# Hybrid layer, output stage: one clearing block less, W_out slots 6 and 7 split by ScalarE and VectorE, order of the first two tiles' projections

## The chip, the cores and the metric

The kernel runs on one core of a Trainium2 chip. The metric is device time in microseconds (us), the median of several runs. A core has five engines with a queue each: TensorE (PE; its weight loads are shown as PEld), VectorE (DVE), ScalarE (ACT), GpSimd (POOL) and SyncE (SP), which here only issues DMAs. They run side by side and wait for one another through semaphores.

## What is computed

One decoder layer on x of 2048 tokens by 1024, in float32:

```python
u  = rmsnorm(x, pre_mix_gain)
p  = u @ w_in                                   # rg_x, rg_gate, q, k, v, o, i, f
y_rg = rmsnorm(rg_lru(conv4(rg_x)) * gelu(rg_gate), rg_out_gain)
y_ml = rmsnorm(sigmoid(o) * mlstm(silu(conv4(q)), silu(conv4(k)), v, i, f), ml_out_gain)
h = x + rmsnorm(concat(y_rg, y_ml) @ w_out, post_mix_gain)
v = rmsnorm(h, pre_mlp_gain)
out = h + rmsnorm(relu(v @ w_up) ** 2 @ w_down, post_mlp_gain)
```

The change touches only the way from y = concat(y_rg, y_ml) to h and v, and what lies between the stages.

## The kernel before

**Stages.** Three parts follow one another: build_prepare (norm, transposes), build_mixers (projection and both mixers, which write y to HBM as a high and a low part) and build_output. Each opens a block of its own with a program for each engine, and a block ends with a barrier of all engines. Behind each of the first two stands clear_semaphores (L1666), a block in which each engine clears a fifth of the semaphores, again with a barrier at its end; then the semaphores are handed out anew.

**Products.** Every product is made of three matmuls: high by high, high by low, low by high (L1350 to L1352, one call each). A float32 weight tile in w_raw is split for it: w_hi is the rounded copy (L1319 on GpSimd, L1520 on ScalarE), w_lo = w_raw - w_hi (L1321). A weight lies in 8 slots of 128 x 1024; slot i uses w_raw[i % 2], so slot i + 2 is loaded (L1297, by GpSimd's queue) when slot i is split.

**Output stage.** It goes twice over 8 token tiles of 128 (B = 0: tiles 0 to 7, B = 1: tiles 8 to 15). Each pass has a projection phase with W_out, then 8 rounds of the MLP (chunk), of which each needs 8 new slots. split_round (L1299) is GpSimd's program for one such set of slots. For B = 0, slots 0 to 5 of W_out were split during the mixers and only 6 and 7 are left to it. For B = 1, slots 4 to 7 are still in use by the last MLP round, so GpSimd does 0 to 3 early; after that round ScalarE makes w_hi of 4 to 7 (L1520), and GpSimd w_lo.

**One tile's projection.** project(B, i, b, part) (L1355) is 24 matmuls: part 0 uses slots 0 to 3 and writes the bank rg_ps, part 1 slots 4 to 7 and ml_ps. It waits for the tile's y (y_in, loaded by SP, L1219), for the slots (w_split) and, last, until its bank has been emptied of the tile before. There is one bank pair for each part. ScalarE empties rg_ps with scale_rg (L1468), which writes h1_t; VectorE empties ml_ps with the sum L1586 (signal "mix"). scale_rg of tile 0 of a pass stands ahead of tile_steps (L1522 in ScalarE's program, behind the high parts of slots 4 to 7 and final_square when B = 1); for each later tile it stands in the middle of the tile before's steps.

**A tile's steps.** VectorE and ScalarE by turns: sum L1586, square sum L1451, root L1456, scale L1593, residual L1599, square sum and root again, v_t (L1607). TensorE transposes v_t (L1374) after the tile after next's part 0, ScalarE copies the high part (L1494), VectorE makes the low part (L1619). In the second pass VectorE and ScalarE also finish the first pass's tiles in between (L1451 on acc, L1564, L1570), SP stores them (L1228) and loads what is needed of the next (L1238), in one queue with the loads of y for the tile after next.

**TensorE's order.** Tiles 0 and 1 of a pass: part 0 and part 1 of tile 0, then of tile 1. Then a loop: part 0 of tile T + 2, transposes of tile T, part 1 of tile T + 2. Then the last transposes and the MLP rounds. GpSimd begins to split the first MLP round's slots when part 0 of the pass's last tile is done.

Of the kernel before, what the change touches and what calls it, by code (L numbers as in the profile page):

```python
# [23 lines left out]
F32 = mybir.dt.float32  # L24
F32R = mybir.dt.float32r
ALU = mybir.AluOpType
ACT = mybir.ActivationFunctionType
# [1116 lines left out]
def build_output(nc, a, k, out):  # L1144
# [4 lines left out]
    NF = DFF // (FC * P)  # L1149
    HALVES = 2  # L1150
    SLOTS = 8
    with ExitStack() as ctx:
# [12 lines left out]
        w_hi = [t[:].rearrange("p k f -> p (k f)") for t in k["w_hi"]] + [sb(f"w_hi{i}", [P, D], F32R)[:] for i in (6, 7)]  # L1165
        w_lo = [t[:].rearrange("p k f -> p (k f)") for t in k["w_lo"]] + [sb(f"w_lo{i}", [P, D], F32R)[:] for i in (6, 7)]
        w_raw = [sb(f"w_raw{i}", [P, D]) for i in range(2)]
# [30 lines left out]
        w_split = [sem(f"w_split{i}") for i in range(SLOTS)]  # L1198
        raw_in = k["raw_in_o"]
# [9 lines left out]
        def raw_count(r, i):  # L1209

            return r * 64 + ((i // 2 + 1) * 16 - 48)
# [68 lines left out]
        @block.gpsimd  # L1280
        def _(pool):
            up = a["mlp_w_up"][0].rearrange("(k p) f -> p k f", p=P)
            down = a["mlp_w_down"][0]
            w_out = a["w_out"][0]

            def source(rnd, f, i):
                if rnd == "out":
                    return w_out[i * P:(i + 1) * P, :]
                if i < FC:
                    return up[:, :, ds(f * (FC * P) + i * P, P)]  # L1290
                return down[ds(f * (FC * P) + (i - FC) * P, P), :]

            def load_raw(rnd, f, i):
                dst = w_raw[i % 2][:]
                if rnd != "out" and i < FC:
                    dst = dst.rearrange("p (k f) -> p k f", k=KT)
                pool.dma_start(dst, source(rnd, f, i)).then_inc(raw_in[i % 2], 16)  # L1297

            def split_round(B, rnd, f):  # L1299
                r = f + (B * (NF + 1) + (rnd != "out"))  # L1300
                first = 6 if rnd == "out" and B == 0 else 0
                load_raw(rnd, f, first)
                load_raw(rnd, f, first + 1)
                for i in range(first, SLOTS):
                    pool.wait_ge(raw_in[i % 2], raw_count(r, i))
                    if rnd == "out":
                        if B and i < FC:
                            pool.wait_ge(s_slot[f"up_used{i}"], s_slot.ready(B * NF - 1))
                        elif B:
                            pool.wait_ge(s_dn["dn_mm"], s_dn.ready(B * NF * 2 * TB - 1))  # L1310
                    else:
                        if i < FC:
                            pool.wait_ge(s["mm_rg"], s.ready(B * TB + TB - 1))
                            pool.wait_ge(s_slot[f"up_used{i}"], f + (B * NF + 1))
                        else:
                            pool.wait_ge(s_y["mm_ml"], s_y.ready(B * TB + TB - 1))
                            pool.wait_ge(s_dn["dn_mm"], (f + B * NF) * (2 * TB) + s_dn.credit)
                    if not (rnd == "out" and B and i >= FC):
                        pool.tensor_tensor(w_hi[i], w_raw[i % 2][:], one_bc, ALU.mult).then_inc(w_split[i], 1)  # L1319
                    pool.wait_ge(w_split[i], r * 2 + 1)  # L1320
                    pool.tensor_tensor(w_lo[i], w_raw[i % 2][:], w_hi[i].bitcast(F32), ALU.subtract  # L1321
                                       ).then_inc(w_split[i], 1)
                    if i + 2 < SLOTS:
                        pool.wait_ge(w_split[i], r * 2 + 2)
                        load_raw(rnd, f, i + 2)
                for i in (SLOTS - 2, SLOTS - 1):
                    pool.wait_ge(w_split[i], r * 2 + 2)

            one_bc = k["one"][:].broadcast_to([P, D])
            for i in range(6):  # L1330
                pool.sem_inc(w_split[i], 2)
            for B in range(NB):
                split_round(B, "out", 0)
                with pool.Fori(0, NF) as f:
                    split_round(B, "mlp", f)

        @block.tensor
        def _(pe):
# [16 lines left out]
            def project(B, i, b, part):  # L1355
                T = i + B * TB
                r = B * (NF + 1)
                bank, evac, done = ((rg_ps, "mix_rg", s["mm_rg"]), (ml_ps, "mix", s_y["mm_ml"]))[part]
                ks = range(part * 4, part * 4 + 4)
                pe.wait_ge(y_in[b], (T // 2 + 1) * 32)  # L1360
                for c in ks:
                    pe.wait_ge(w_split[c], r * 2 + 2)
                pe.wait_ge(s[evac], s.freed(T))
                for h in range(HALVES):
                    cols = slice(h * 512, (h + 1) * 512)
                    last = product(bank[:, h, :], [(y_hi[b][:, c, :], y_lo[b][:, c, :], w_hi[c][:, cols],
                                                    w_lo[c][:, cols]) for c in ks])
                last.then_inc(done, 1)
# [45 lines left out]

            for B in range(NB):
                T0 = B * TB
                for i in range(2):
                    project(B, i, i, 0)
                    project(B, i, i, 1)
                if B:  # L1420
                    pe.wait_ge(s_dn["add"], s_dn.ready(B * NF * 16 - 1))
                with pe.Fori(0, TB // 2 - 1) as j:
                    for b in range(2):
                        i = j * 2 + (2 + b)
                        project(B, i, b, 0)
                        transposes(j * 2 + (T0 + b))
                        project(B, i, b, 1)
                transposes(T0 + TB - 2)

                def last_transposes():  # L1430
                    transposes(T0 + TB - 1)

                    pe.wait_ge(s["sq2"], s.ready(T0 + TB - 1))

                chunk(B, 0, last_transposes)
                with pe.Fori(1, NF) as f:
                    chunk(B, f)

        @block.scalar
        def _(act):  # L1440
# [70 lines left out]
            act.wait_ge(rg_scale, 1)  # L1511
            nc.scalar.activation(stat["s_rg"][:], stat["t_rg"][:], ACT.Sqrt).then_inc(rg_scale, 1)
            act.wait_ge(rg_scale, 3)
            for B in range(NB):
                if B:
                    act.wait_ge(s_dn["add"], s_dn.ready(B * NF * 16 - 1))

                    for i in range(FC, SLOTS):
                        act.wait_ge(raw_in[i % 2], raw_count(B * (NF + 1), i))
                        nc.scalar.activation(w_hi[i], w_raw[i % 2][:], ACT.Copy).then_inc(w_split[i], 1)  # L1520
                    final_square(B - 1, 0)
                scale_rg(B, 0, 0)  # L1522
                tile_steps(B, 0, 0, before=False)
                with act.Fori(0, TB // 2 - 1) as j:
                    for b in (1, 0):
                        tile_steps(B, j * 2 + (1 if b else 2), b)
                tile_steps(B, TB - 1, 1, after=False)
                tile_evac(B, TB - 1)
                for b in range(2):
                    act.wait_ge(h1_out[b], (B + 1) * (TB // 2) * 16)  # L1530
                if B:
                    ready("fo", B * TB - 1)
                with act.Fori(0, NF) as f:
                    chunk(B, f)
# [8 lines left out]
        def _(dve):  # L1543
# [105 lines left out]
            dve.wait_ge(rg_scale, 2)  # L1649
            nc.vector.reciprocal(stat["s_rg"][:], stat["s_rg"][:]).then_inc(rg_scale, 1)  # L1650
            for B in range(NB):
                tile_steps(B, 0, 0, before=False)
                with dve.Fori(0, TB // 2 - 1) as j:
                    for b in (1, 0):
                        tile_steps(B, j * 2 + (1 if b else 2), b)
                tile_steps(B, TB - 1, 1)
                tile_evac(B, TB - 1)
                if B:
                    dve.wait_ge(fin_out, 16 * TB)
                chunk(B, 0, True)  # L1660
                with dve.Fori(1, NF if B < NB - 1 else NF - 1) as f:
                    chunk(B, f, False)
# [39 lines left out]
def hybrid_layer(nc, a, out):  # L1702
    with ExitStack() as ctx:
# [46 lines left out]
        with ExitStack() as sems:  # L1750
            k["sems"] = sems
            build_mixers(nc, a, k)
            clear_semaphores(nc, k)
        mixer_consts.close()
        with ExitStack() as sems:
            k["sems"] = sems
            build_output(nc, a, k, out)


# [17 lines left out]
```

## Time and profile before

| what | us |
|---|---|
| median of 3 runs (2466.47 to 2467.31) | 2466.69 |
| the profiled execution | 2467.44 |
| its span | 2465.6 |
| TensorE busy | 2335.1 (95%) |
| VectorE busy | 1278.3 (52%) |
| GpSimd busy | 834.4 (34%) |
| ScalarE busy | 642.5 (26%) |

The mixers end at 822.8 us of the span, the first pass's projections run from 835.1 to about 957, its MLP rounds to 1634; the second pass's projections from 1634 (with a gap) to about 1777, its MLP rounds to 2456. Times in the rows are in us from the span's start. In rows of the timeline the second column is the duration, and the square brackets at the end tell how long the engine was idle before, and what ended that. Matmuls are pipelined, so their durations overlap.

### The profile page before, as it was taken

How to read it: one execution, taken by the hardware profiler on the slowest of the kernel's cores; microseconds unless marked ns; L12 is line 12 of the kernel's file. 1: busy time of each engine (PE TensorE's matmuls, PEld its weight loads, DVE VectorE, ACT ScalarE, POOL GpSimd, SP SyncE). 2: the span in 40 equal slices, each digit the busy share in tenths (PEclk: the TensorE clock that was granted, in tenths of full speed). 3: DMA queues.
4: the chain of work that ended last, by engine and by line, in shares of the span. 5: the costliest groups of instructions: out<-in, count | busy, mean ns of one | idle time of the engine just before them, and what ended most of it. 6: DMA issues, size and time to landing. Idle time of an engine off the chain costs nothing.

```text
span 2465.6 us, 29981 instructions
## 1 busy us (share of the span) xinstructions
PE 2335.1 (95%) x10696; PEld 1943.9 (79%) x10696; DVE 1278.3 (52%) x1584; ACT 642.5 (26%) x1159; POOL 834.4 (34%) x486
## 2 busy tenths in 40 slices
PE   5779999999999599999999999979899999999998
PEld 5758888888887487888888888868688888888886
DVE  5345665656656256445435444517755434534535
ACT  3315554545545232001101101114201101100112
POOL 8400000000000108536435534610746534633630
PEclk9689999999999799999999999989899999999999
DMA  4634453635542552112111101327412111101203
GB/s 171 245 119 153 149 190 121 218 122 174 165 165 71 170 163 94 43 52 68 34 43 60 51 34 51 102 98 244 144 51 69 43 42 51 60 27 50 68 17 145
DMA packets 125177, 254.85 MB, mean 103 GB/s; under 512 B 8105, under 2 KB 43137, under 8 KB 125121
## 3 DMA queue, kind: packets, MB, share of 16 engines
q1 hardware_dynamic: 97008, 157.37, 19.0%
q0 software_dynamic: 24320, 88.35, 11.4%
q10 hardware_dynamic: 3792, 8.47, 0.9%
q8 instruction: 24, 0.39, 0.1%
q14 instruction: 33, 0.26, 0.0%
HBM read 201.67 MB, written 50.40 MB: 102 GB/s over the span
## 4 chain that ended last, share of the span: by engine, by line
PE 60%; DVE 3%; issue 1%; ACT 1%; DMA 1%; POOL 0%; ACTq 0%; DVEq 0%; SPq 0%; PEldq 0%; POOLq 0%
PE o_ps L1350 20%; PE o_ps L1352 20%; PE o_ps L1351 20%; DVE o_relu L1626 1%; DVE o_ff_lo L1630 1%; ACT o_ps L1451 1%; PE o_ps L1374 0%; DMA o_v_lo<-ylo_d 0%; DVE o_acc L1570 0%; DVE o_v_lo L1619 0%; DMA o_w_raw<-in_w_out 0%; DVE o_h_t L1586 0%; ACT o_ff_hi L1508 0%; DVE o_h_t L1599 0%; DVE o_v_t L1607 0%
## 5 line engine op out<-in xcount | busy, mean ns | idle before, releaser
L1319 POOL TENSOR_TENSOR w_hi<-o_w_raw,one 128x1024 fp32r<-128x1024 f32 x100 | 191.7, 1917 | 685.2 <-PE o_ps L1352 594.7
L1350 PE MATMUL o_ps<-o_v_hi,w_hi 128*128 128x512 f32 x1024 | 400.1, 391 | 4.8 <-DVE o_v_lo L1619 4.8
L1351 PE MATMUL o_ps<-o_v_lo,w_hi 128*128 128x512 f32 x1024 | 399.6, 390 | 0.0
L1352 PE MATMUL o_ps<-o_v_hi,w_lo 128*128 128x512 f32 x1024 | 399.6, 390 | 0.0
L1640 DVE TENSOR_TENSOR o_acc<-o_ps,o_acc 128x512 f32<-128x512 f32 x224 | 154.2, 690 | 377.5 <-PE o_ps L1352 377.2
L658 PE MATMUL m_unit_ps<-u_hi,w_hi 128*128 128x512 f32 x768 | 309.4, 403 | 6.3 <-issue 6.3
L1626 DVE TENSOR_TENSOR o_relu<-o_relu 128x512 f32<-128x512 f32 x128 | 218.8, 1710 | 182.7 <-ACT o_relu L1505 181.7
L1505 ACT ACTIVATE o_relu<-o_ps 128x512 f32<-128x512 f32 x128 | 76.5, 597 | 874.9 <-PE o_ps L1352 843.3
L658 PE MATMUL m_unit_ps<-u_hi,w_lo 128*128 128x512 f32 x768 | 301.5, 393 | 0.0
L658 PE MATMUL m_unit_ps<-u_lo,w_hi 128*128 128x512 f32 x768 | 299.9, 390 | 0.0
L1630 DVE TENSOR_TENSOR o_ff_lo<-o_relu,o_ff_hi 128x512 fp32r<-128x512 f32 x128 | 243.1, 1899 | 90.8 <-ACT o_ff_hi L1508 90.8
L1321 POOL TENSOR_TENSOR w_lo<-o_w_raw,w_hi 128x1024 fp32r<-128x1024 f32 x102 | 274.1, 2688 | 47.2 <-ACT w_hi L1520 39.4
L1350 PEld LDWEIGHTS o_ps<-o_v_hi,w_hi 128*128 128x128 f32 x1024 | 193.1, 189 | 45.4 <-issue 5.3
L1352 PEld LDWEIGHTS o_ps<-o_v_hi,w_lo 128*128 128x128 f32 x1024 | 193.0, 188 | 40.2
L1351 PEld LDWEIGHTS o_ps<-o_v_lo,w_hi 128*128 128x128 f32 x1024 | 193.0, 189 | 40.1
L1350 PE MATMUL o_ps<-w_hi,o_ff_hi 128*128 128x512 f32 x512 | 199.3, 389 | 1.4 <-DVE o_acc L1637 1.4
L1352 PE MATMUL o_ps<-w_hi,o_ff_lo 128*128 128x512 f32 x512 | 199.2, 389 | 0.0
L1350 PE MATMUL o_ps<-o_w_hi,o_ff_hi 128*128 128x512 f32 x512 | 199.2, 389 | 0.0
L1352 PE MATMUL o_ps<-o_w_hi,o_ff_lo 128*128 128x512 f32 x512 | 199.2, 389 | 0.0
L1351 PE MATMUL o_ps<-o_w_lo,o_ff_hi 128*128 128x512 f32 x512 | 199.2, 389 | 0.0
L1351 PE MATMUL o_ps<-w_lo,o_ff_hi 128*128 128x512 f32 x512 | 199.2, 389 | 0.0
L615 POOL DMA_DIRECT2D w_raw<-in_w_in x18 | 15.9, 885 | 482.6 <-DVE w_lo L1075 462.4
(255 smaller groups left out, 3639.5 us busy)
## 6 DMA issues: line engine op xcount, KB each, us to landing
o_w_raw<-in_mlp_w_up POOLq DMA_DIRECT2D x64, 512.0 KB, 4.7
o_w_raw<-in_mlp_w_down POOLq DMA_DIRECT2D x64, 512.0 KB, 3.6
u_hi<-uhi_d SPq DMA_DIRECT2D x14, 2048.0 KB, 10.6
u_lo<-ulo_d SPq DMA_DIRECT2D x14, 2048.0 KB, 15.0
w_raw<-in_w_in POOLq DMA_DIRECT2D x24, 512.0 KB, 4.8
p_xu<-in_x SPq DMA_DIRECT2D x16, 512.0 KB, 7.9
uhi_d<-u_hi SPq DMA_DIRECT2D x4, 2048.0 KB, 7.5
ulo_d<-u_lo SPq DMA_DIRECT2D x4, 2048.0 KB, 13.1
```

What stands on the lines that cost most here:

```text
L615: pool.dma_start(w_raw[c % 3][:], w_view[:, :, ds(g * P + W_COL[UNITS[c]], P)]).then_inc(raw_in[c % 3], 16)
L658: last = nc.tensor.matmul(unit_bank[u][:], w[u][:, c, :], x[:, b, c, :], start=(c == 0 and z == 0), stop=(c == KT - 1 and z == 2))
L1319: pool.tensor_tensor(w_hi[i], w_raw[i % 2][:], one_bc, ALU.mult).then_inc(w_split[i], 1)
L1321: pool.tensor_tensor(w_lo[i], w_raw[i % 2][:], w_hi[i].bitcast(F32), ALU.subtract).then_inc(w_split[i], 1)
L1350: nc.tensor.matmul(dst, sh, mh, start=(i == 0), stop=False)
L1351: nc.tensor.matmul(dst, sh, ml, start=False, stop=False)
L1352: last = nc.tensor.matmul(dst, sl, mh, start=False, stop=(i == n - 1))
L1451: nc.scalar.activation(junk, src, ACT.Square, accum_out=stat["ss" + n][:, ds(T, 1)]).then_inc(s["sq" + n], 1)
L1505: nc.scalar.activation(relu[n % 2][:], ps[:, n % 4, :], ACT.Relu).then_inc(s_up["relu"], 1)
L1626: nc.vector.tensor_tensor(relu[n % 2][:], relu[n % 2][:], relu[n % 2][:], ALU.mult).then_inc(s_ff["ffsq"], 1)
L1630: nc.vector.tensor_tensor(ff_lo[:, i, cols], relu[n % 2][:], ff_hi[:, i, cols].bitcast(F32), ALU.subtract).then_inc(s_ff["fflo"], 1)
L1640: nc.vector.tensor_tensor(dst, ps[:, 4 + n % 4, :], dst, ALU.add).then_inc(s_dn["add"], 1)
```

## The change

Three things are changed. The clearing block behind the mixers is gone: the output stage takes new semaphores beside those of the mixers. In both rounds of W_out GpSimd leaves slots 6 and 7 alone (it still loads them and waits until they are split); ScalarE makes the high part (new for B = 0, as before for B = 1) and VectorE the low part, ahead of its first tile. And TensorE projects part 0 of tiles 0 and 1 of a pass, then part 1 of both.

```diff
--- before.py
+++ after.py
@@ -1302,6 +1302,9 @@
                 load_raw(rnd, f, first)
                 load_raw(rnd, f, first + 1)
                 for i in range(first, SLOTS):
+                    if rnd == "out" and i >= SLOTS - 2:
+                        pool.wait_ge(w_split[i], r * 2 + 2)
+                        continue
                     pool.wait_ge(raw_in[i % 2], raw_count(r, i))
                     if rnd == "out":
                         if B and i < FC:
@@ -1414,9 +1417,9 @@
 
             for B in range(NB):
                 T0 = B * TB
-                for i in range(2):
-                    project(B, i, i, 0)
-                    project(B, i, i, 1)
+                for part in range(2):
+                    for i in range(2):
+                        project(B, i, i, part)
                 if B:
                     pe.wait_ge(s_dn["add"], s_dn.ready(B * NF * 16 - 1))
                 with pe.Fori(0, TB // 2 - 1) as j:
@@ -1511,6 +1514,9 @@
             act.wait_ge(rg_scale, 1)
             nc.scalar.activation(stat["s_rg"][:], stat["t_rg"][:], ACT.Sqrt).then_inc(rg_scale, 1)
             act.wait_ge(rg_scale, 3)
+            for i in (SLOTS - 2, SLOTS - 1):
+                act.wait_ge(raw_in[i % 2], raw_count(0, i))
+                nc.scalar.activation(w_hi[i], w_raw[i % 2][:], ACT.Copy).then_inc(w_split[i], 1)
             for B in range(NB):
                 if B:
                     act.wait_ge(s_dn["add"], s_dn.ready(B * NF * 16 - 1))
@@ -1649,6 +1655,10 @@
             dve.wait_ge(rg_scale, 2)
             nc.vector.reciprocal(stat["s_rg"][:], stat["s_rg"][:]).then_inc(rg_scale, 1)
             for B in range(NB):
+                for i in (SLOTS - 2, SLOTS - 1):
+                    dve.wait_ge(w_split[i], B * (NF + 1) * 2 + 1)
+                    nc.vector.tensor_tensor(w_lo[i], w_raw[i % 2][:], w_hi[i].bitcast(F32), ALU.subtract
+                                            ).then_inc(w_split[i], 1)
                 tile_steps(B, 0, 0, before=False)
                 with dve.Fori(0, TB // 2 - 1) as j:
                     for b in (1, 0):
@@ -1750,10 +1760,7 @@
         with ExitStack() as sems:
             k["sems"] = sems
             build_mixers(nc, a, k)
-            clear_semaphores(nc, k)
-        mixer_consts.close()
-        with ExitStack() as sems:
-            k["sems"] = sems
+            mixer_consts.close()
             build_output(nc, a, k, out)
```

## Rows read from the trace of the kernel before

**Rows 1.** The page, part 1: busy time of the engines.
```profile
PE 2335.1 (95%) x10696; PEld 1943.9 (79%) x10696; DVE 1278.3 (52%) x1584; ACT 642.5 (26%) x1159; POOL 834.4 (34%) x486
```

**Rows 2.** Table by stretches: length, busy time per engine, granted clock, DMA share, GB/s.
```profile
840.00:845.00 5.00, 5.00 (x22) 4.13 (x21) 0.00 (x0) 1.12 (x1) 2.58 (x3) 0.94 1.01 379
...
955.00:960.00 5.00, 2.58 (x13) 2.01 (x12) 3.01 (x2) 2.11 (x4) 4.25 (x4) 1.00 0.30 105
...
1646.00:1652.00 6.00, 0.00 (x0) 0.00 (x0) 0.00 (x0) 4.15 (x5) 4.51 (x2) 0.50 0.20 80
```

**Rows 3.** Lines of both barriers and TensorE's clears: count, ns min/median/max, starts.
```profile
L500 SPq EVENT_SEMAPHORE  x1: 17/17/17, 822.8 to 822.8; - x1
...
L1669 PEldq DRAIN  x2: 13/13/13, 139.0 to 825.1; - x2
L1669 SPq EVENT_SEMAPHORE  x2: 17/17/17, 139.2 to 825.3; - x2
...
L1688 PEldq EVENT_SEMAPHORE_RANGE_CLEAR  x25: 56/56/63, 138.2 to 825.0; - x25
```

**Rows 4.** Timeline, start of the output stage: start, duration, engine, line, operation.
```profile
825.86 0.58 SPq L1219 DMA_DIRECT2D o_v_hi<-yhi_d  x1
...
828.70 3.40 SPq L1219 DMA_DIRECT2D o_v_lo<-ylo_d  x1
...
835.09 0.79 PE L1350 MATMUL o_ps<-w_hi,o_v_hi 128*128 128x512 f32 x1 [16.89 <-DMA o_v_lo<-ylo_d]
...
838.38 2.36 POOL L1321 TENSOR_TENSOR o_w_lo<-o_w_raw,o_w_hi 128x1024 fp32r<-128x1024 f32 x1
```

**Rows 5.** Timeline, tiles 0 and 1 of the first pass.
```profile
843.51 1.12 ACT L1468 ACTIVATE o_h_t<-o_ps,o_s_rg 128x1024 f32<-128x1024 f32 x1 [15.80 <-PE o_ps L1352]
...
848.99 1.23 DVE L1586 TENSOR_TENSOR o_h_t<-o_ps,o_h_t 128x1024 f32<-128x1024 f32 x1 [20.99 <-PE o_ps L1352]
...
853.38 1.23 DVE L1599 TENSOR_TENSOR o_h_t<-o_h_t,o_xh 128x1024 f32<-128x1024 f32 x1
...
857.13 1.29 DVE L1607 SCALAR_TENSOR_TENSOR o_v_t<-o_h_t,o_rs,o_pre_mlp 128x1024 f32<-128x1024 f32 x1
859.76 1.23 DVE L1586 TENSOR_TENSOR o_h_t<-o_ps,o_h_t 128x1024 f32<-128x1024 f32 x1 [1.35 <-PE o_ps L1352]
```

**Rows 6.** Timeline between the passes: ScalarE, GpSimd, TensorE.
```profile
1648.53 1.06 ACT L1520 ACTIVATE o_w_hi<-o_w_raw 128x1024 fp32r<-128x1024 f32 x1 [1.21 <-DMA o_w_raw<-in_w_out]
...
1650.53 1.09 ACT L1468 ACTIVATE o_h_t<-o_ps,o_s_rg 128x1024 f32<-128x1024 f32 x1
...
1647.49 4.64 POOL L1321 TENSOR_TENSOR o_w_lo<-o_w_raw,o_w_hi 128x1024 fp32r<-128x1024 f32 x2 [4.84 <-ACT o_w_hi L1520]
...
1652.39 0.77 PE L1350 MATMUL o_ps<-w_hi,o_v_hi 128*128 128x512 f32 x1 [12.84 <-POOL o_w_lo L1321]
```

**Rows 7.** Timeline, tiles 8 and 9: VectorE's first sums, ScalarE's wait.
```profile
1660.12 1.23 DVE L1586 TENSOR_TENSOR o_h_t<-o_ps,o_h_t 128x1024 f32<-128x1024 f32 x1 [25.19 <-PE o_ps L1352]
...
1665.46 1.12 ACT L1468 ACTIVATE o_h_t<-o_ps,o_s_rg 128x1024 f32<-128x1024 f32 x1 [2.42 <-PE o_ps L1352]
...
1670.90 1.23 DVE L1586 TENSOR_TENSOR o_h_t<-o_ps,o_h_t 128x1024 f32<-128x1024 f32 x1 [0.21 <-PE o_ps L1352]
```

**Rows 8.** Timeline, end of the second pass's projections, all engines.
```profile
1723.41 0.82 SPq L1219 DMA_DIRECT2D o_v_lo<-ylo_d  x1
...
1730.00 0.49 PE L1350 MATMUL o_ps<-w_hi,o_v_hi 128*128 128x512 f32 x1 [0.21 <-DMA o_v_lo<-ylo_d]
...
1733.82 1.22 DVE L1586 TENSOR_TENSOR o_h_t<-o_ps,o_h_t 128x1024 f32<-128x1024 f32 x1
...
1735.97 1.89 POOL L1319 TENSOR_TENSOR w_hi<-o_w_raw,one 128x1024 fp32r<-128x1024 f32 x1 [81.22 <-PE o_ps L1352]
...
1739.14 3.14 DVE L1599 TENSOR_TENSOR o_h_t<-o_h_t,o_xh 128x1024 f32<-128x1024 f32 x1
...
1750.34 1.94 PE L1374 MATMUL o_ps<-ident,o_v_t 128*128 128x128 f32 x8 [8.24 <-DVE o_v_lo L1619]
```

## The prediction

> **Names.** A token tile is 128 tokens; tiles 0 to 7 are the first pass of the output stage (B = 0), tiles 8 to 15 the second (B = 1). The first half of a tile's projection is slots 0 to 3 of W_out into the rg bank, the second half slots 4 to 7 into the ml bank. 0.2% of 2466.7 us is 4.9 us, about what a measurement of this kernel can tell from no change.
>
> **What bounds the kernel now.** I read the page first: TensorE is busy 95% of the span [rows 1], so only a place where it waits, or a wait that the change adds, can move the time. Then the waits of PE and the table by stretches [rows 2], then the timeline around each place that the diff touches. Three places matter. (1) Between the mixers and the output stage TensorE is idle for 16.89 us, and its first matmul waits for the DMA of tile 0's low part, not for a weight slot [rows 4]. (2) Between the passes it is idle for 12.84 us, until GpSimd has split slot 7 [rows 6]. (3) After that the second pass is set by the chain of VectorE and ScalarE, one tile in (1733.82 - 1670.90) / 5 = 12.58 us [rows 7, 8], which ends in 8.24 us of idle TensorE ahead of tile 14's transposes [rows 8]. In the first pass VectorE waits for TensorE at each tile (1.35 us at tile 1) [rows 5], so there TensorE sets the pace. The MLP rounds are TensorE's, and nothing in them is touched.
>
> **Part 1, the clearing block.** SP leaves the mixers' barrier at 822.8 and the clearing block's at 825.3; TensorE is the late one, 25 clears of 56 ns each over both blocks and a drain at 825.1 [rows 3]. Nothing computes in that time and the loads of the output stage begin 0.5 us after it, at 825.86 [rows 4]. All DMA of the mixers has landed (the barrier follows the wait for it), so the loads find the same empty queues, only earlier. Price: -2.5 us. Bounds: 0, if what follows were held by something else, and -2.5.
>
> **Part 2, slots 6 and 7 in the first pass.** GpSimd ends its last split at 838.38 + 2.36 = 840.7 [rows 4]; the slots are first needed at the second half of tile 0, after 843.5 [rows 5]. The split by ScalarE (1.06 us for the high part of a slot [rows 6]) and VectorE (1.23 us for a sum of two 128x1024 tiles in SBUF [rows 5]) ends sooner, about 834, in both engines' idle time. Price: 0. GpSimd gets free earlier and loads the first two MLP tiles (1 MB) among SP's loads; tile 1's low part, asked for at 828.7, must now be there at about 842 instead of 849, with over 10 us in hand.
>
> **Part 3, the order of the halves in the first pass.** Each bank holds one tile. Before, TensorE left the rg bank, worked 5.5 us on the ml bank (843.51 to 848.99), and the rg bank had long been emptied when it came back. Now the first half of tile 1 comes right behind that of tile 0 and must wait until ScalarE has emptied the bank: 1.12 us [rows 5] and some 0.15 us for the two hand-overs = 1.3 us. In the same way the second half of tile 1 comes right behind that of tile 0 and waits for VectorE's sum: 1.23 us [rows 5] + 0.15 us = 1.4 us. These 2.7 us lie on TensorE, which sets the pace of this pass: +2.7 us. (The 0.15 us are an estimate, of which the lower bound is 0 and the upper the 0.26 us that TensorE took to start behind GpSimd's split, 1652.39 - (1647.49 + 4.64) [rows 6].) Tile 0's sum is now 5.5 + 2.7 us later against TensorE's start, so its chain to v_t, 848.99 to 858.42 [rows 5], ends at about 862.5; its transposes come at about 865.6, so this costs nothing, and VectorE's delay of 2 us at tile 1 melts by some 0.3 us a tile, since TensorE is the slower one. First pass together: -2.5 + 2.7 = +0.2 us.
>
> **Part 4, the second pass.** This is where I expect the loss. ScalarE's program is: high parts of slots 4 to 7, the square of the last accumulated tile, and only then the emptying of the rg bank, 1650.53 to 1651.62 [rows 6]. The first half of tile 8 was done at 1652.4 - 12.8 = 1639.6 [rows 6] and sits in that bank. So the first half of tile 9, now second in line, can't start before about 1651.7: it can't use the 12 idle us. And since it stands ahead of the second half of tile 8, whose slots are ready at 1650.9 (ScalarE ends slot 7's high part at 1649.59 [rows 6], VectorE needs 1.23 us instead of GpSimd's 2.35), it delays it. The gain of the faster split, 1652.1 - 1650.9 = 1.2 us, is not used either.
> Sum: the first project after the idle stretch runs partly at the lower clock and takes 1660.12 - 1652.39 = 7.7 us [rows 6, 7]; the next 5.5 us. Second half of tile 8 done: 1651.7 + 7.7 + 5.5 = 1664.9 instead of 1660.1, +4.8 us. VectorE's chain of tile 8, and with it the whole chain of this pass, begins 4.8 us later. Two things are taken back. VectorE's 0.21 us wait ahead of tile 9's sum goes [rows 7]; and ScalarE no longer sits 2.42 us in front of tile 9's bank [rows 7], since that half is finished early, which brings tile 8's second square some 0.3 us forward. +4.8 - 0.5 = +4.3 us. Bounds: +3.8 (the same chain with 1 us of slack found) and +4.8.
> The wait for tile 8's sum ahead of tile 9's second half (1.4 us) is hidden here, since the chain is the slower one. Does the +4.3 reach the end? TensorE has no lead in this pass that could grow: tile 15's first half waited 0.21 us for a load [rows 8] that SP issues behind the store of a final tile, so behind VectorE's chain. It moves by the same 4.3 us, and with it GpSimd's first MLP split, 1735.97, which follows that half. So VectorE's chain meets GpSimd in the same phase as before, tile 14's transposes come at 1750.34 + 4.3 (+0.2), and from there TensorE sets the pace to the end, as before.
>
> **Sum.** +0.2 + 4.3 = +4.5 us. The profiled execution has a span of 2465.6 and took 2467.4, 1.8 us around it; it is 0.75 us above the median of the runs. Span after: 2470.1, its time about 2472.0. On the median: 2466.7 + 4.5 = **2471.2 us**, +0.18%, just inside the bound of 4.9 us.
>
> **Where the port between VectorE and GpSimd comes in.** A VectorE sum with both inputs in SBUF, 1.23 us alone, took 3.14 us while GpSimd split a slot [rows 5, 8]. If the tile-15 half did not wait for its load, GpSimd would start 2 us earlier against VectorE's chain; stepping through the rows with whole instructions blocking one another, tile 14's v_t then ends anywhere from 2.1 to 4.8 us later than before, instead of 4.3. The Trainium skill, page "SBUF — State Buffer", section "Who interferes with whom", says that such a VectorE instruction and one of GpSimd that reads SBUF exclude each other for a whole instruction, and that issue order decides who waits; the 3.14 us agree.
>
> **Rivals.**
> (a) Slower by over 0.2%: the same mechanism, a little dearer. The first project of the output stage ran some 13 matmuls at the lower clock (835.09 to 840.4) [rows 4, 2], the one at 1652.39 only 9 or 10, at 0.20 us each. If tile 9's first half gets 13, +0.8 us; if the 0.5 us of slack do not come, +0.5 us. 2471.7 to 2472.5. It decides from 0.4 us on. For: the terms are only known to a few tenths, and all that remains open in part 4 is slack. Against: the first pass may in turn save 0.8 us. Chance 0.27.
> (b) The clearing block was cover for something, such as loads or instruction code, and the first matmul does not move: +7.0 us, 2473.7. For: TensorE's wait ends with a DMA. Against: that DMA is issued 0.5 us after the barrier. Chance 0.06.
> (c) The two stalls of 1.3 us in the first pass come just after the clock has risen, and it falls again: 24 matmuls of a half at 0.20 us more each, +4.8 us, 2476.0. Against: from 955 to 960 TensorE was idle 2.4 of 5 us and the granted clock stayed at 1.00 [rows 2]. Chance 0.05. The Trainium skill, page "TensorE: Matmul & The Clock Gate", section "A second HAM failure mode: psum-queue depth-cycling", tells of short idle times between groups of matmuls, from cycling through PSUM banks, between which the clock went up and down; the row of 955 to 960 does not agree, so the case keeps a small chance.
> (d) The port's phase is kinder, as above: +2.3 instead of +4.5, 2469.0. Needs the load of tile 15 to be early. Chance 0.12.
> (e) The change does what its order suggests: tile 9's first half runs in the idle stretch, and tile 8's second half starts at 1651.0 at the upper clock. Then -1.4 - 2.2 + 0.2 = -3.4 us, 2463.3. Against: the place of the bank's emptying in ScalarE's program. Chance 0.04; faster by over 0.2% needs still more, 0.04.
> Forecast 0.42.
>
> **How the numbers follow.** Within 0.2%: forecast, (d), (e) = 0.58. Slower: (a), (b), (c) = 0.38. Faster: 0.04. Range: from (d) with 0.4 us less to just past (b): 2468.6 to 2474.0. It leaves out (c), (e) and the faster case, 0.13, and strays.
>
> **What would show it.** First load of the output stage at 823.4. TensorE idle 1.3 us behind the first half of tile 0, for ScalarE's emptying, and 1.4 us behind its second half, for VectorE's sum. Between the passes TensorE idle about 12.2 us, ended by ScalarE's emptying of the rg bank, not by a split, and VectorE's first sum of the pass some 4.8 us later against the end of the first pass. Wrong, if tile 9's first half starts before 1651, if the wait at 1651.7 is ended by a weight slot, or if the gap ahead of tile 14's transposes takes up the loss.

## The result

| kernel | median us | runs | ratio of its runs to before | 95% interval |
|---|---|---|---|---|
| before | 2467.86 | 15 | | |
| changed | 2471.69 | 15 | 1.0017 | 1.0009 to 1.0025 |
| changed, measured again (e9) | 2471.88 | 11 | 1.0022 | 1.0013 to 1.0031 |

The change costs 3.8 us by the medians, 2.2 to 6.2 by the interval of the first comparison: slower beyond the noise, by about 0.2%; on which side of 0.2% it lies, neither interval tells. The prediction was +4.5 us.

The profiled execution of the changed kernel is one of the slowest: 2475.64 us, span 2473.9, which is 8.3 us above that of before. So the two traces are compared from two points that the change does not touch: R, the mixers' last root (L844, 815.89 before, 817.85 after), and E, VectorE's last accumulation of a pass's MLP rounds (1634.23 before, 1638.58 after).

**Where TensorE waits after.** The waits of TensorE in the changed kernel from 1600 on (engine, line, who it waited for: us in total, times, longest), then its waiting rows of the first pass in the timeline, with ScalarE's and VectorE's that end them:

```profile
PE o_ps L1353 <- ACT o_h_t L1471: 12.2, 1, 12.2
PE o_ps L1377 <- DVE o_v_lo L1625: 8.3, 1, 8.3
PE o_ps L1353 <- DVE o_v_lo L1625: 2.4, 1, 2.4
PE o_ps L1353 <- DMA o_v_lo<-ylo_d: 2.0, 4, 0.8
PE o_ps L1353 <- DVE o_h_t L1592: 1.5, 1, 1.5
```

```profile
825.35 0.59 SPq L1219 DMA_DIRECT2D o_v_hi<-yhi_d  x1
...
834.52 0.80 PE L1353 MATMUL o_ps<-w_hi,o_v_hi 128*128 128x512 f32 x1 [14.35 <-DMA o_v_lo<-ylo_d]
...
841.63 0.39 PE L1355 MATMUL o_ps<-w_hi,o_v_lo 128*128 128x512 f32 x1
843.31 0.47 PE L1353 MATMUL o_ps<-w_hi,o_v_hi 128*128 128x512 f32 x1 [1.30 <-ACT o_h_t L1471]
843.62 0.40 PE L1354 MATMUL o_ps<-w_lo,o_v_hi 128*128 128x512 f32 x1
...
855.96 0.47 PE L1353 MATMUL o_ps<-w_hi,o_v_hi 128*128 128x512 f32 x1 [1.51 <-DVE o_h_t L1592]
...
842.05 1.11 ACT L1471 ACTIVATE o_h_t<-o_ps,o_s_rg 128x1024 f32<-128x1024 f32 x1 [7.43 <-PE o_ps L1355]
...
854.59 1.23 DVE L1592 TENSOR_TENSOR o_h_t<-o_ps,o_h_t 128x1024 f32<-128x1024 f32 x1 [18.70 <-PE o_ps L1355]
```

The first load stands 7.5 us behind R (825.35 - 817.85) instead of 10.0, the first matmul 16.7 instead of 19.2 [rows 4]. Then come two waits that before did not have [rows 5]: 1.30 us until ScalarE has emptied the rg bank, 1.51 us until VectorE's sum has emptied the ml bank. TensorE loses more than these idle times, because matmuls in a row overlap: they start 0.23 us apart, across the first wait 843.31 - 841.63 = 1.68 us, and the next one comes 0.31 us later. That is 1.5 us for the first wait, and in the same way 1.8 us for the second (854.06 to 855.96 and 856.26): 3.3 us for the two.

**Between the passes and at the end of the second.** Timeline rows, as in [rows 6 to 8]:

```profile
1654.86 1.09 ACT L1471 ACTIVATE o_h_t<-o_ps,o_s_rg 128x1024 f32<-128x1024 f32 x1
...
1653.95 1.22 DVE L1660 TENSOR_TENSOR o_w_lo<-o_w_raw,o_w_hi 128x1024 fp32r<-128x1024 f32 x1 [0.91 <-ACT o_w_hi L1526]
...
1656.10 0.77 PE L1353 MATMUL o_ps<-w_hi,o_v_hi 128*128 128x512 f32 x1 [12.21 <-ACT o_h_t L1471]
...
1669.63 1.22 DVE L1592 TENSOR_TENSOR o_h_t<-o_ps,o_h_t 128x1024 f32<-128x1024 f32 x1 [14.46 <-PE o_ps L1355]
...
1679.81 1.22 DVE L1592 TENSOR_TENSOR o_h_t<-o_ps,o_h_t 128x1024 f32<-128x1024 f32 x1
...
1738.83 0.49 PE L1353 MATMUL o_ps<-w_hi,o_v_hi 128*128 128x512 f32 x1 [0.30 <-DMA o_v_lo<-ylo_d]
...
1742.73 1.22 DVE L1592 TENSOR_TENSOR o_h_t<-o_ps,o_h_t 128x1024 f32<-128x1024 f32 x1
...
1744.80 1.89 POOL L1322 TENSOR_TENSOR w_hi<-o_w_raw,one 128x1024 fp32r<-128x1024 f32 x1 [87.00 <-PE o_ps L1355]
...
1759.17 1.94 PE L1377 MATMUL o_ps<-ident,o_v_t 128*128 128x128 f32 x8 [8.28 <-DVE o_v_lo L1625]
```

TensorE's gap is hardly shorter (12.21 us for 12.84), and it is no longer a weight slot that ends it but ScalarE's emptying of the rg bank. Slot 7 was ready at 1653.95 + 1.22 = 1655.17, 0.9 us before TensorE went on. VectorE's first sum of the pass stands 31.05 us behind E instead of 25.89, its sum of tile 14 104.15 instead of 99.59, tile 14's transposes 120.59 instead of 116.11.

### The profile page after: what moved, and what is told of

Read it like the earlier page. It is cut to its first block and busy times, and to the rows that moved or that the text cites. A ratio compares the mean times of both kernels' runs of the same rounds, so it can differ in the third digit from the quotient of the medians.

```text
span 2473.9 us, 29879 instructions
## 1 busy us (share of the span) xinstructions
PE 2339.0 (95%) x10696; PEld 1945.7 (79%) x10696; DVE 1287.7 (52%) x1588; ACT 644.6 (26%) x1161; POOL 820.6 (33%) x480
```

## Experiments

All distances are read from rows as above: P1 is from R to the last low part of v in the first pass (140.4 us before), M the first pass's MLP rounds from there to E (678.0), S8 from E to VectorE's first sum of the second pass (25.9), T14 from E to tile 14's transposes (116.1). Each kernel has one profile, so a distance is one reading; between kernels that do the same in a stretch, P1 differs by up to 0.6 us and T14 by up to 0.7.

| kernel | P1 | M | S8 | T14 | median us | before beside it | ratio (95%) |
|---|---|---|---|---|---|---|---|
| before | 140.4 | 678.0 | 25.9 | 116.1 | | | |
| changed | 140.4 | 680.4 | 31.0 | 120.6 | 2471.7 | 2467.9 | 1.0017 (1.0009 to 1.0025) |
| e9 changed again | 140.6 | 678.3 | 30.9 | 120.3 | 2471.9 | 2467.7 | 1.0022 (1.0013 to 1.0031) |
| e1 block only | 136.6 | 678.2 | 25.6 | 115.8 | 2465.3 | 2467.5 | 0.9991 (0.9982 to 0.9999) |
| e2 split only | 139.9 | 678.0 | 24.9 | 115.3 | 2466.1 | 2467.5 | 0.9995 (0.9986 to 1.0003) |
| e3 order only (5 runs) | 143.4 | 677.4 | 31.2 | 120.6 | 2474.2 | 2467.5 | 1.0036 (1.0023 to 1.0049) |
| e4 block and split | 136.7 | 678.3 | 25.1 | 115.2 | 2464.7 | 2467.5 | 0.9989 (0.9980 to 0.9997) |
| e5 change, early emptying | 140.0 | 678.3 | 24.9 | 114.8 | 2467.3 | 2467.3 | 0.9996 (0.9987 to 1.0004) |
| e6 as e5, old order in pass 1 | 137.1 | 680.0 | 25.5 | 115.9 | 2464.6 | 2467.3 | 0.9988 (0.9979 to 0.9996) |
| e7 change, new order in pass 2 alone | 137.0 | 678.2 | 30.4 | 119.9 | 2469.3 | 2467.3 | 1.0008 (1.0000 to 1.0017) |
| e8 change, new order in pass 1 alone | 140.0 | 680.4 | 25.4 | 115.7 | 2467.0 | 2467.3 | 0.9998 (0.9989 to 1.0007) |
| e10 change, y asked for early | 140.1 | 678.3 | 30.8 | 121.0 | 2473.0 | 2467.7 | 1.0021 (1.0012 to 1.0030) |

### The three parts alone

**The clearing block** (e1). Edit:

```diff
             build_mixers(nc, a, k)
-            clear_semaphores(nc, k)
-        mixer_consts.close()
-        with ExitStack() as sems:
-            k["sems"] = sems
+            mixer_consts.close()
             build_output(nc, a, k, out)
```

> Only the clearing block behind the mixers is gone, all else as before. My theory: the first load of the output stage is issued 2.5 us earlier against the end of the mixers, tile 0's low part lands as much earlier, TensorE paces the first pass, and the kernel is 2.5 us faster (-0.10%). Rival (the block covers loads or instruction code): the first matmul of the output stage does not move against the mixers' end, 0 us. In the profile, the time from the mixers' last root (L844) to the first matmul of the output stage is 19.2 us before; 16.7 by the theory, 19.2 by the rival.

Measured: -2.2 us by the medians. The first load stands 825.43 - 817.94 = 7.5 us behind R, as my theory has it; the rival's 19.2 us to the first matmul fell, it is 15.8:

```profile
825.43 0.59 SPq L1219 DMA_DIRECT2D o_v_hi<-yhi_d  x1
826.07 0.66 SPq L1219 DMA_DIRECT2D o_v_lo<-ylo_d  x1
...
833.74 0.79 PE L1350 MATMUL o_ps<-w_hi,o_v_hi 128*128 128x512 f32 x1 [13.49 <-DMA o_v_lo<-ylo_d]
```

That is 3.4 us earlier, not 2.5: the rest is the load of tile 0's low part itself, which took from its issue to the first matmul 833.74 - 826.07 = 7.7 us here and 835.09 - 826.49 = 8.6 us before. P1 gained 3.8 us. The 0.4 us left is the clock: behind the first matmul TensorE starts at the lower clock (granted 0.50, a matmul each 0.43 us instead of 0.23), and 10 matmuls ran at it here, 12 before.

**The split** (e2). Edit: the parts of the diff in split_round, in ScalarE's and in VectorE's program; nothing else.

> Only slots 6 and 7 are split by ScalarE and VectorE; the clearing block and TensorE's order stay. My theory: nothing in the first pass; between the passes slot 7 is ready at VectorE's 1.23 us behind its high part instead of GpSimd's 2.35, so TensorE's gap of 12.84 us shrinks to about 11.5 and the kernel is 1.3 us faster (-0.05%). Rival: GpSimd's earlier loads of MLP tiles get in the way of tile 1's y, or the slower of the two engines decides: 0 or a little slower.

Measured: -1.4 us by the medians, with an interval that holds 0, so the total can't be told from none; the rows can. TensorE's gap between the passes is 0.9 us shorter, S8 1.0 us and T14 0.8 us. That is less than the 1.3 expected of the gap (11.5 us), but the rival fell: the gap is shorter and P1, 139.9, is not longer:

```profile
1652.68 0.77 PE L1353 MATMUL o_ps<-w_hi,o_v_hi 128*128 128x512 f32 x1 [11.95 <-DVE o_w_lo L1660]
```

**The order** (e3). Edit:

```diff
-                for i in range(2):
-                    project(B, i, i, 0)
-                    project(B, i, i, 1)
+                for part in range(2):
+                    for i in range(2):
+                        project(B, i, i, part)
```

> Only TensorE's order is changed. My theory: +2.7 us in the first pass (1.3 us behind ScalarE's emptying, 1.4 us behind VectorE's sum, both shown as waits of TensorE) and +4.3 us in the second, since the first half of tile 9 waits for ScalarE's emptying until about 1651.7 and then stands ahead of tile 8's second half: together +7.0 us (+0.28%). Rival (the first half of tile 9 hides in the gap between the passes): TensorE's gap is cut by 5.5 us and the second pass gains, in all +1 us or less.

Measured: +6.7 us by the medians; P1 +3.0, T14 +4.5. TensorE's waiting rows, first pass and second:

```profile
844.08 0.47 PE L1350 MATMUL o_ps<-w_hi,o_v_hi 128*128 128x512 f32 x1 [1.36 <-ACT o_h_t L1468]
856.74 0.47 PE L1350 MATMUL o_ps<-w_hi,o_v_hi 128*128 128x512 f32 x1 [1.51 <-DVE o_h_t L1586]
```

```profile
1653.62 0.77 PE L1350 MATMUL o_ps<-w_hi,o_v_hi 128*128 128x512 f32 x1 [11.89 <-ACT o_h_t L1468]
1668.98 0.47 PE L1350 MATMUL o_ps<-w_hi,o_v_hi 128*128 128x512 f32 x1 [1.51 <-DVE o_h_t L1586]
```

The rival fell: nothing of the gap was used. All of the change's loss, and more, is the order of the halves.

**Block and split together** (e4; the edits of e1 and e2).

> The clearing block gone and the split moved, TensorE's order as before. My theory, if the parts add: -2.5 - 1.3 = -3.8 us (-0.15%), faster than both kernels. Rival (the parts depend on one another, the order is needed for the split to pay): about -2.5 us or less.

Measured: -2.8 us by the medians, P1 -3.7, T14 -0.9. By the rows the parts add to within 0.5 us (-4.2 on P1 and -1.1 on T14 from e1 and e2); in the medians they would add to -3.5, which the intervals can't tell from -2.8. It is faster than before by its interval, and the changed kernel is slower than before by its own.

### Is it the place of the emptying in ScalarE's program?

**Emptying early** (e5). The whole change, and:

```diff
                         nc.scalar.activation(w_hi[i], w_raw[i % 2][:], ACT.Copy).then_inc(w_split[i], 1)
+                        if i == FC + 1:
+                            scale_rg(B, 0, 0)
                     final_square(B - 1, 0)
-                scale_rg(B, 0, 0)
+                else:
+                    scale_rg(B, 0, 0)
```

> The whole change, but ScalarE empties the rg bank of tile 8 right behind the high parts of slots 4 and 5, ahead of those of 6 and 7. My theory: tile 9's first half now runs in the idle stretch between the passes (start about 6.6 us behind the last down product's sum instead of 17.5), tile 8's second half starts when slot 7 is split (about 17.2), and VectorE's first sum of the second pass comes 22.3 to 24.9 us behind that point, by how cold the clock is (31.05 in the changed kernel, 25.89 before). The whole kernel: the loss of 4.3 us in the second pass becomes a gain of 1 to 3.5, so 1 to 3.4 us below before (-0.04 to -0.14%) and 5 to 8 us below the change. Rival (something else holds tile 9's first half, its y or a slot): sum and time as in the changed kernel, +4 us.

The mechanism is as I had it: tile 9's first half now follows tile 8's after 1.30 us, inside what was the gap, and S8 falls from 31.0 to 24.9 us:

```profile
1643.41 0.47 PE L1353 MATMUL o_ps<-w_hi,o_v_hi 128*128 128x512 f32 x1 [1.30 <-ACT o_h_t L1471]
1654.44 0.76 PE L1353 MATMUL o_ps<-w_hi,o_v_hi 128*128 128x512 f32 x1 [5.34 <-DVE o_w_lo L1663]
1663.02 0.47 PE L1353 MATMUL o_ps<-w_hi,o_v_hi 128*128 128x512 f32 x1 [1.51 <-DVE o_h_t L1595]
```

Against the change that is 4.4 us by the medians (5 to 8 expected); against before nothing that the measurement can tell (1 to 3.4 us faster expected). Two things were less than I thought. The half that now runs early brings nothing by itself: the pass's chain starts with tile 8's second half, which still waits for slot 7, and S8 is the same as with the old order and the same split (24.9 here, 25.1 in e4). And the lower clock stayed: behind the 5.34 idle us TensorE again began at it, for 6 matmuls here and, behind 4.47 idle us, for 13 in e6 (9 in e4, whose gap is 11.99 us). The table by stretches (length, busy time by engine, granted clock, DMA share, GB/s):

```profile
1650.00:1655.00 5.00, 0.56 (x1) 0.50 (x2) 2.24 (x2) 2.10 (x3) 0.00 (x0) 0.89 0.12 48
1655.00:1660.00 5.00, 5.00 (x19) 4.00 (x18) 0.00 (x0) 0.00 (x0) 1.80 (x2) 0.77 0.62 195
```

**The same with the old order in the first pass** (e6):

```diff
-                for part in range(2):
-                    for i in range(2):
-                        project(B, i, i, part)
+                order = ((0, 0), (1, 0), (0, 1), (1, 1)) if B == 1 else ((0, 0), (0, 1), (1, 0), (1, 1))
+                for i, part in order:
+                    project(B, i, i, part)
```

> As the run before, but the first pass keeps the old order of halves. My theory: it also saves the two waits of TensorE in the first pass (2.7 to 3 us), so it is the fastest of all, 4 to 6 us below before (-0.16 to -0.24%). Rival (the first pass has slack that hides the two waits): equal to the run before.

Measured: -2.7 us by the medians, the lowest with e4, and less than the 4 to 6 expected, for the reasons just named. P1 is 2.9 us below e5's, so the first pass has no slack that hides the two waits: the rival fell.

**The new order in one pass alone** (e7: as e6 without the early emptying; e8: the same with `B == 0`).

> The change with the new order in the second pass alone. My theory: -2.5 us (block), -0.4 (split), +4.3 to +4.5 in the second pass: +1.5 us (+0.06%). In the profile the stretch from the mixers' last root to the last low part of the first pass is 136.6 us as in the runs with the block gone and the old order, and VectorE's first sum of the second pass stands 31 us behind the first pass's last.

> The change with the new order in the first pass alone. My theory: -2.5 (block) + 2.7 to 3 (order) in the first pass, so that stretch is about 140 us, and in the second the split's gain, VectorE's first sum 25 us behind the first pass's last: -0.7 us in all (-0.03%). Rival (GpSimd's early MLP loads, not the order, cost the first pass its gain): this stretch would be 140 us in the run before too.

e7: +2.0 us by the medians, P1 137.0, S8 30.4. e8: -0.3 us, P1 140.0, S8 25.4. The two losses are separate and lie where they were put: about 3 us in the first pass (P1 140.0 in e8, 137.0 in e7), 4 to 5 in the second (T14 119.9 in e7, 115.7 in e8). What ends the gap between the passes changes with the order, first e7, then e8:

```profile
1650.35 0.76 PE L1353 MATMUL o_ps<-w_hi,o_v_hi 128*128 128x512 f32 x1 [12.15 <-ACT o_h_t L1471]
```

```profile
1654.51 0.77 PE L1353 MATMUL o_ps<-w_hi,o_v_hi 128*128 128x512 f32 x1 [11.59 <-DVE o_w_lo L1660]
```

e8's rival fell with e7, whose GpSimd loads MLP tiles as early as e8's and whose P1 is 137.0.

### Does the load of y tie GpSimd to VectorE's chain?

**The changed kernel again** (e9, no edit).

> The changed kernel once more, for a second profile. The first one had a span of 2473.9 us, 4 us above the median run. My theory: 2.0 us of that lie ahead of the output stage and 2.4 us at the first down product of the first MLP round, where TensorE waited 2.2 us and the granted clock was 0.66 for 5 us; both are accidents of that execution, while the +5.2 us at VectorE's first sum of the second pass is not. So in a second profile that sum again stands 31.0 us (30.4 to 31.3) behind the first pass's last, and the time is 2471 to 2472. Rival (the change itself makes that wait longer): the wait at the first down product is again 2.2 us and the stretch of the first pass's MLP rounds 680.4 instead of 678.0 us.

The sum again stands 30.95 us behind E, T14 is 120.3, M 678.3 and not 680.4, and the time 2471.9. So the 2 us ahead of R and the 2 us in M of the first profile don't belong to every execution of the change. Kernels without it have them too: R lies at 815.7 to 816.1 in four of the twelve profiles and at 817.2 to 818.4 in eight, e1 and e4 among these.

**y asked for early** (e10). The changed kernel, and in SP's program (tile 2's y is asked for ahead of the loop, the last two tiles are written out behind it):

```diff
-                load_y(B, i + 2, b)
                 load_x(B, i + 2, b)
+                load_y(B, i + 3, 1 - b)
                 finished(B, i)
```

> The changed kernel, but SP asks for the y of a tile as soon as its buffer is free, not behind the store of a final tile. My theory: in the second pass TensorE no longer waits for that load, so tile 15's first half and with it GpSimd's first MLP split come about 2 us earlier against VectorE's chain, and GpSimd and VectorE meet in another phase: tile 14's transposes move by -2.2 to +0.5 us against the changed kernel's 120.6 us behind the first pass's last sum, with VectorE's sum of tile 14 unmoved at 104.2. Time: -2 to +0.5 us against the changed kernel. Rival (the load's wait does not pace GpSimd, or the phase does not matter): no wait for y in the second pass, tile 14's transposes at 120.6, the same time.

TensorE's waits for y in the second pass are gone, and GpSimd's first split stands 0.2 us behind VectorE's sum of tile 14 instead of 2.1 (1744.80 - 1742.73 in the changed kernel). Timeline:

```profile
1740.55 1.89 POOL L1326 TENSOR_TENSOR w_hi<-o_w_raw,one 128x1024 fp32r<-128x1024 f32 x1 [84.41 <-PE o_ps L1359]
...
1740.36 1.22 DVE L1596 TENSOR_TENSOR o_h_t<-o_ps,o_h_t 128x1024 f32<-128x1024 f32 x1
...
1743.95 2.06 DVE L1603 SCALAR_TENSOR_TENSOR o_h_t<-o_h_t,o_rs,o_post_mix 128x1024 f32<-128x1024 f32 x1
...
1757.56 1.94 PE L1381 MATMUL o_ps<-ident,o_v_t 128*128 128x128 f32 x8 [10.11 <-DVE o_v_lo L1629]
```

VectorE's scaling of tile 14 now meets GpSimd for longer (2.06 us; 1.47 in the changed kernel, 1.28 where GpSimd is idle), and from its sum to the transposes it is 1757.56 - 1740.36 = 17.2 us instead of 16.4. So the load did pace GpSimd, and a GpSimd that starts 1.9 us earlier makes this stretch 0.8 us longer, not shorter: the first rival point, "the phase does not matter", fell, but by less than a microsecond, and on one profile each. The median is 1.1 us above that of e9, beyond the +0.5 expected, but with these intervals the total can't be told from the changed kernel's.

## Why the prediction came out right, point by point

- **Clearing block, -2.5 us.** Right: 7.5 us (once 7.6) for 10.0 to 10.2 from R to the first load, in all nine profiles without the block. The landing of y that follows adds or takes up to 0.9 us by execution (first matmul 15.8 to 16.7 us behind R with the block gone).
- **Split in the first pass, 0.** Right within the scatter; P1 is 139.9 and 140.4, and e4's P1 is that of e1.
- **The two waits in the first pass, 1.3 and 1.4 us.** Right as idle times, 1.30 and 1.51, but too small as a cost: TensorE lost 3.3 us, not 2.7. Compared with kernels of the old order that had as many matmuls at the lower clock, the stretch from the first matmul to the last low part of v is 3.1 to 3.4 us longer. VectorE's delay behind the waits melted, as foreseen: its sums stood 6.2 us later behind the first matmul at tile 0, 4.5 at tile 1, 2.5 from tile 6 on. The 5.5 + 2.7 us that the prediction gives for tile 0's sum holds one wait too many (the second comes behind that sum); its 862.5 fits 5.5 + 1.3.
- **First pass together, +0.2.** P1 is 0.0 and +0.2 us in the two profiles, in part by luck. In the first, -2.5 from the earlier start, +3.3 from the waits and -0.8 because 8 matmuls ran at the lower clock instead of 12 (it rose 3.6 us behind the first matmul; 5.3 before). In e9, -3.0, +3.3 and -0.2 (11 matmuls).
- **The second pass, +4.8 at its start.** Right in mechanism and in size: the gap is ended by ScalarE's emptying, S8 is +5.2 and +5.1 us in the two profiles of the change. From E to the start of tile 9's first half it is 17.5 and 18.0 us for 17.5, and the two halves then took 13.5 and 13.0 us for 7.7 + 5.5; 11 matmuls ran at the lower clock in the first, 8 in e9, 9 before.
- **-0.5 us of slack behind it.** From tile 8's sum to tile 9's it is 10.18 us instead of 10.78, so -0.6.
- **No more lost or gained up to tile 14.** T14 is +4.5 and +4.2 for +4.3. GpSimd's first split met VectorE's chain in the same phase, 2.1 us behind tile 14's sum for 2.15 [rows 8]; e10 shows that the load of y is what holds it there, and that with an early load the phase is not kinder, as rival (d) had it, but 0.4 us worse on T14.
- **The rivals.** (a), the same loss but above 0.2%, is not excluded by either interval. (b), a block that covers something, fell with e1. (c), the clock falling behind the two stalls, did not come: the granted clock was 1.00 from 840 on. But the row that the prediction held against it, TensorE idle for 2.4 us at 957 with the clock at 1.00 behind it, does not hold in every execution (see the last section). (e), the hidden half, came only when the emptying was moved (e5), and there T14 is 1.3 us below before, of which e4 has 0.9 without it. My error about it was that I let tile 8's second half start at 16.8 us behind E at the upper clock; in e5 it started at 17.6, with 6 matmuls at the lower one.
- **Sum.** +4.5 predicted; +3.8 and +4.2 by the medians, 1.0017 and 1.0022 by the ratios. By the rows of e9, whose span is 3.9 us above that of before, it is +0.2 on P1, +0.4 on M, +4.2 on T14 and -0.8 behind T14, where 714.4 us were left instead of 715.3. The last two small terms, M and the rest behind T14, were not in the prediction and nearly cancel; in the first profile they are +2.4 and -0.5. The rest behind T14 is 713.7 to 715.7 us in the twelve profiles, and no run shows what sets it.

## What to carry to other kernels

Ahead of moving work into an idle stretch, look for every buffer it writes and for where the engine that empties that buffer has the emptying in its program; here, with one bank for each kind of product, two products of a kind in a row cost one emptying each time, 1.30 us by ScalarE or 1.51 by VectorE, and 0.2 us more than that in TensorE's starts. Of an idle stretch ask what starts the chain behind it: the half that e5 moved into the gap wasn't on that chain and gave nothing that could be measured, and in the change, put ahead of the chain's first link, its 5.5 us cost 4.7 (T14 in e7 and e4). And the barrier, with idle engines on both sides, was worth its full 2.5 us, the surest term of this change.

## What was not expected

In its two comparisons the changed kernel scatters more: 2466.1 to 2475.6 us over 15 runs, before 2465.9 to 2468.9. That is no fixed property of the two: beside e5 to e8 before itself ranged from 2462.1 to 2470.1 us over 35 runs, as widely as e7 and e8. A part of the scatter was seen. TensorE waits for VectorE's first accumulation of the first MLP round, 0 to 2.2 us in the twelve profiles. In three profiles of twelve the granted clock fell behind it, and M was 680.0 to 680.4 us instead of 677.4 to 678.3: in both with a wait of 2.2 us (changed, e8) and in one (e6) of the three with 1.8. The stretch in the first profile of the change:

```profile
990.00:995.00 5.00, 2.81 (x13) 2.00 (x12) 4.30 (x4) 0.63 (x1) 4.31 (x3) 1.00 0.39 105
995.00:1000.00 5.00, 5.00 (x16) 3.94 (x15) 2.08 (x4) 0.00 (x0) 4.25 (x4) 0.66 0.31 105
```

In 5 us at a mean clock of 0.66 TensorE began 16 matmuls instead of 24, about 1.6 us lost. The wait of 2.42 us some 35 us earlier [rows 2], for v's last low part, left the clock at 1.00 in ten profiles, before and after the change among them. In e2 and e5 the clock fell behind it; the row of e2:

```profile
960.00:965.00 5.00, 5.00 (x17) 3.95 (x16) 4.22 (x3) 1.11 (x2) 4.38 (x3) 0.66 0.30 105
```

There M is 678.0 and 678.3 us all the same, probably because TensorE came later to the wait for VectorE: that was 0 and 0.2 us. So the same wait can leave the clock up or bring it down from one execution to the next, and a single profile does not exclude the fall. Whether this is what makes the changed kernel scatter was not tested: executions without a profile don't show it.
